# Shared expert of the last two token tiles moved behind the expert loop, and expert 0's weights requested at the head of the output stage

## The reference

```
h   = layer_norm(ALPHA * h + mixer_out @ w_out, ln1_g, ln1_b)      # per token
idx, w = route(h)                                # 6 of 64 experts per token, with weights
routed = sum over the chosen experts e of  w_e * ((silu(h @ wg[e]) * (h @ wu[e])) @ wd[e])
shared = (silu(h @ sg) * (h @ su)) @ sd          # one expert for all tokens
out = layer_norm(ALPHA * h + routed + shared, ln2_g, ln2_b)
```

## Time and profile before

| | us |
|---|---|
| median of 3 runs | 2063.84 (2063.03 to 2066.24) |
| the profiled execution | 2066.02 |
| its span in the profile | 2064.2 |
| PE busy | 1989.3 (96%) |
| DVE busy | 1136.6 (55%) |
| ACT busy | 505.2 (24%) |
| POOL busy | 777.1 (38%) |

### The profile page before, as it was taken

How to read it: one execution, slowest core, us unless ns; L and a number is a source line. 1 busy time by engine, 2 the same in 40 slices (tenths; PEclk the granted TensorE clock), 3 DMA queues, 4 the chain that set the end, 5 groups by cost and what they waited for, 6 DMA issues and landing times.

```text
span 2064.2 us, 23774 instructions
## 1 busy us (share of the span) xinstructions
PE 1989.3 (96%) x7237; PEld 1004.3 (49%) x7238; DVE 1136.6 (55%) x3065; ACT 505.2 (24%) x1102; POOL 777.1 (38%) x717
## 2 busy tenths in 40 slices
PE   8999999999999999999999999999999999999991
PEld 6444667575544444444445554444444444444440
DVE  6222546776611222235676656966666656666645
ACT  3111554452322222224432230111111111111113
POOL 1762005612122222115980003554554545454531
PEclk9999999999999999999999999999999999999996
DMA  5421000011141222144353006999999999999964
GB/s 147 132 87 41 21 21 22 22 47 47 46 138 69 74 77 77 57 130 161 111 202 141 31 32 260 369 364 359 360 360 354 364 346 354 347 342 352 337 206 171
DMA packets 129639, 370.45 MB, mean 179 GB/s; under 512 B 33712, under 2 KB 65668, under 8 KB 103832
## 3 DMA queue, kind: packets, MB, share of 16 engines
q1 hardware_dynamic: 103960, 314.83, 41.1%
q0 software_dynamic: 23520, 54.61, 10.5%
q10 hardware_dynamic: 2080, 0.01, 0.1%
HBM read 320.57 MB, written 68.17 MB: 188 GB/s over the span
## 4 chain that ended last, share of the span: by engine, by line
PE 25%; DMA 21%; issue 4%; POOL 3%; DVE 2%; POOLq 0%; ACT 0%; SPq 0%; DVEq 0%
DMA sums<-arena,row_to 21%; PE banks L3193 8%; PE banks L2289 4%; PE banks L3209 3%; PE banks L2336 3%; POOL arena L2136 2%; PE banks L2014 2%; PE banks L279 1%; PE banks L2352 1%; PE banks L2312 1%; DMA arena<-in_w_router_dram 0%; DVE arena L3269 0%; PE banks L3201 0%; DVE arena L3186 0%; PE banks L2299 0%
## 5 line engine op out<-in xcount | busy, mean ns | idle before, releaser
L3193 PE MATMUL banks<-arena 128*128 128x512 f32 x1056 | 466.6, 595 | 4.1 <-issue 3.5
L3172 POOL DMA_INDIRECT arena<-h_rows,index x268 | 281.0, 1048 | 140.2 <-issue 78.7
L3193 PEld LDWEIGHTS banks<-arena 128*128 128x128 f32 x1056 | 196.6, 191 | 227.7 <-issue 227.6
L1720 PE MATMUL banks<-arena 128*128 128x512 f32 x672 | 298.8, 594 | 0.4 <-ACT arena L323 0.4
L3209 PE MATMUL banks<-arena 128*128 128x512 f32 x528 | 237.5, 592 | 1.4 <-ACT arena L3008 0.9
L3180 POOL DMA_INDIRECT sums<-arena,row_to x66 | 106.2, 1609 | 275.9 <-DMA sums<-arena,row_to 242.2
L279 PE MATMUL banks<-arena 128*128 128x512 f32 x416 | 193.5, 602 | 2.3 <-PEq L108 2.2
L1720 PEld LDWEIGHTS banks<-arena 128*128 128x128 f32 x672 | 123.2, 190 | 134.7 <-issue 134.7
L3156 DVE TENSOR_SCALAR index<-row 32x1 uint32<-32x1 f32 x1072 | 155.4, 145 | 17.1
L3209 PEld LDWEIGHTS banks<-arena 128*128 128x128 f32 x528 | 100.2, 190 | 127.1 <-issue 125.3
L3186 DVE STREAM_TRANSPOSE arena<-arena 128x1024 f32<-128x1024 f32 x66 | 133.7, 2026 | 48.9 <-PE banks L3193 47.2
(11 more groups left out here) (400 smaller groups left out, 2420.0 us busy)
## 6 DMA issues: line engine op xcount, KB each, us to landing
arena<-in_w_exp_gate_dram SPq DMA_DIRECT2D x66, 1024.0 KB, 6.4
arena<-in_w_exp_up_dram SPq DMA_DIRECT2D x66, 1024.0 KB, 10.7
arena<-in_w_exp_down_dram SPq DMA_DIRECT2D x66, 1024.0 KB, 13.5
arena<-in_w_in_dram SPq DMA_DIRECT2D x26, 1024.0 KB, 5.4
gates<-arena SPq DMA_DIRECT2D x60, 256.0 KB, 2.0
arena<-gates SPq DMA_DIRECT2D x15, 1024.0 KB, 7.7
arena<-h_rows,index POOLq DMA_INDIRECT x268
arena<-in_x_dram SPq DMA_DIRECT2D x8, 512.0 KB, 5.6
```

The costliest lines, as they stand in the source:

```text
L1720: mm = pe.matmul(gate_bank(n, b), left[:, k, :], right[:, k, :], start=(alone and k == 0), stop=(k == 3), skip_group_check=True)
L3172: return pool.indirect_dma_start(w.x[k][:, 256 * q:256 * (q + 1)], None, rows, bass.IndirectOffsetOnAxis(ap=g.index[:, k, q:q + 1], axis=0 ...
L3193: mm = pe.matmul(g.bank[:, 2, :].rearrange("p (a f) -> p a f", a=2), xT[:, k, :], wgu[:, :, k, :], start=(k == 0), stop=(k == KT - 1))
```

## The change

`EARLY` is 6. Four things change.

First, the shared expert of tiles 6 and 7 leaves the output stage. Their turned rows are kept in the rows of `base` of tiles 0 and 1, which must have been stored by then (`kept_free`). ACT scales tiles 6 and 7 by ALPHA (`scale`), and SP stores the scaled rows to `sums`. In the final stage PE makes the two tiles: `up` when the last list is there, before the last scatter has landed; then it adds the loaded rows of `sums` in PSUM through a product with the identity matrix, and the `down` products on top. ACT reads these two tiles from PSUM.

Second, SP asks for expert 0's weights ahead of all stores of the output stage, and waits for tile 6 instead of 8 of the shared expert ahead of experts 2 and 3.

Third, the order at the start of the loop is new on PE and DVE. Up of tile 5 is cut in two by the list of expert 0. In step 0 DVE turns expert 1's rows and makes `hidden` ahead of `index`.

Fourth, since the shared weights must stay in `R1` until the end, the overflow tables and the rows of `ln2` lie in the rows of `base` of tiles 2 to 7. So DVE waits ahead of the tables, and SP ahead of loading `ln2`, until all of these have been stored to `sums`.

```diff
@@ norm_and_route, SP
+        load_expert(g, sp, 0)
         for m in range(NT):
             keep_rows(m)
             if m > DELAY:
                 begin_sum(m - DELAY - 1)
         sp.wait_ge(s["mix"], NT)
-        for e in range(2):
-            load_expert(g, sp, e)
-        for m in range(NT - DELAY - 1, NT - 2):
+        load_expert(g, sp, 1)
+        begin_sum(NT - DELAY - 1)
+        for m in range(EARLY, NT):
             begin_sum(m)
-        sp.wait_ge(s["gu"], NT)
+        sp.wait_ge(s["gu"], EARLY)
         load_expert(g, sp, 2)
-        begin_sum(NT - 2)
-        sp.wait_ge(s["dn"], NT)
+        begin_sum(EARLY - 2)
+        sp.wait_ge(s["dn"], EARLY)
         load_expert(g, sp, 3)
-        begin_sum(NT - 1)
+        begin_sum(EARLY - 1)
@@ norm_and_route, PE
-        up(5)
+        up(5, range(0, KT // 2))
         lists(0)
+        up(5, range(KT // 2, KT))
         down(4)
         turn_hidden(5)
-        up(6)
         lists(1)
-        down(5)
-        turn_hidden(6)
-        up(7)
         lists(2)
-        down(6)
-        turn_hidden(7)
-        first.last_down = lambda: down(NT - 1)
+        first.last_down = lambda: down(EARLY - 1)
@@ experts, SP
             first.sync(sp)
+            sp.wait_ge(g.sums_begun, 16 * EARLY)
@@ experts, DVE, step
-                if has(i, c, -1):
+                if not has(i, c, -1):
+                    turned(i, c + 1)
+                    hidden(i, c)
+                    index(i, c + 3)
+                    select(i, c + 4)
+                else:
                     take_rows(i, c - 1)
...
                 if isinstance(i, int) and i == 0:
+                    dve.wait_ge(g.sums_begun, 16 * EARLY)
                     overflow_tables(g, dve, c, then, s["tabled"])
@@ finish, PE (new)
+        pe.wait_ge(v["list"], count)
+        for m in late:
+            for k in range(KT):
+                mm = pe.matmul(bank[:, up_bank[m], :], late_turned(g, m)[:, k, :], wgu[:, k, :],
+                               start=(k == 0), stop=(k == KT - 1))
+            mm.then_inc(s["gu"], 1)
+        for i, m in enumerate(late):
+            pe.wait_ge(s["hid"], i + 1)
+            for k in range(2):
+                mm = pe.transpose(bank[:, up_bank[m], k * P:(k + 1) * P], hid[:, k * P:(k + 1) * P], g.ident[:])
+            mm.then_inc(s["hT"], 1)
+            pe.wait_ge(sum_in[m], 32)
+            for h in range(2):
+                pe.matmul(bank[:, sum_bank[m] + h, :], g.ident[:], z(m)[:, h * HALF:(h + 1) * HALF],
+                          start=True, stop=False)
+            pe.wait_ge(s["hTr"], i + 1)
...
+            mm.then_inc(s["dn"], 1)
@@ finish, ACT
+        late_gate(0)
         for m in range(1, NT):
-            act.wait_ge(sum_in[m], 16)
+            if m == 2:
+                late_gate(1)
+                late_hidden(0)
+            if m == 4:
+                late_hidden(1)
+            if m < EARLY:
+                act.wait_ge(sum_in[m], 32)
+            else:
+                act.wait_ge(s["dn"], m - EARLY + 1)
```

More of the change, by code:

```diff
@@ L2219, in norm_and_route @@
     h1_stored = [sem(f"h1_stored{m}") for m in range(NT)]
+    kept_free = [sem(f"kept_free{i}") for i in range(NT - EARLY)]
     g.sums = nc.dram_tensor("sums", [T, D], F32, kind="Internal").ap()
@@ L2235, in mix_bank @@
         return 6 if m == 1 else 0
-    h_in = [sem(f"h_in{m}") for m in range(NT)]
+    h_in = g.rows_in = [sem(f"rows_in{m}") for m in range(NT)]
     def sync(sp):
@@ L2328, in count, with up @@
             mm.then_inc(s["cnt"], 1)
-        def up(m):
+        def up(m, part=range(KT)):
             if m:
@@ L2334, in up @@
                 pe.wait_ge(s["w"], 48)
-            for k in range(KT):
+            for k in part:
                 mm = pe.matmul(bank[:, up_bank[m], :], h1T(m)[:, k, :], wgu[:, k, :],
                                start=(k == 0), stop=(k == KT - 1))
-            mm.then_inc(s["gu"], 1)
+            if k == KT - 1:
+                mm.then_inc(s["gu"], 1)
         def turn_hidden(m):
@@ L2532, in vector @@
         sum_base(3)
+        index(0)
         hidden(5)
-        index(0)
         select(1)
         sum_base(4)
-        hidden(6)
         index(1)
         select(2)
-        sum_base(5)
         turned_first()
+        index(2)
         select(3)
[L2543 to L2546, removed]
+        first.last_sum = lambda: sum_base(EARLY - 1)
     def scalar(act):
@@ L2588, in scalar @@
         gate(4)
+        for m in range(EARLY, NT):
+            scale(m)
         turned_hidden(4)
@@ L2827, in before @@
                 first.tensor(pe, lambda b: lists(0, b))
-                lists(0, 3)
             def step(i, c):
                 up(i, c)
+                if not has(i, c, -2):
+                    lists(i, c + 3)
                 if has(i, c, -1):
@@ L2835, in step @@
                     first.last_down()
-                if has(i, c, 4):
+                if has(i, c, 4) and has(i, c, -1):
                     lists(i, c + 4)
@@ L2937, in step @@
             def step(i, c):
-                if has(i, c, -1):
-                    take_rows(i, c - 1)
[L2940 to L2946, removed]
+                if not has(i, c, -1):
[4 more added lines that the diff above has]
+                else:
+                    take_rows(i, c - 1)
+                    if has(i, c, 3):
+                        index(i, c + 3)
+                    if has(i, c, 4):
+                        select(i, c + 4)
+                    if has(i, c, 1):
+                        turned(i, c + 1)
+                    hidden(i, c)
                 if has(i, c, -1):
@@ L3119, in expert_work @@
     g.over, g.ovend, g.ones64, g.iota48 = take(NE), take(NE), take(NE), take(48)
-    g.ovef, g.idle, g.ovmore = (g.region(R1 + 3072 + 48 * i, 48) for i in range(3))
+    g.ovef, g.idle, g.ovmore = (g.region(TABLES + 3072 + 48 * i, 48) for i in range(3))
     w.list, w.flag = g.list, g.flag
@@ L3214, in scale_rows, with late_turned, finish @@
 def scale_rows(g):
[L3215 to L3221 removed]
+    return g.region(SCALES, D), g.region(SCALES + D, D)
+def late_turned(g, m):
+    return g.region(KEPT + D * (m - EARLY), KT, P)
+def finish(g, v, ended):
+    sem, bank = g.sem, g.bank
+    at = RING[3] + 2 * D
+    silu, hid, hidT = g.region(at, FF), g.region(at + FF, FF), g.region(at + 2 * FF, 2, P)
+    wgu, wdn = g.region(SHARED, KT, 512), g.region(SHARED + 4096, 2, D)
+    late = range(EARLY, NT)
+    up_bank = {EARLY: 1, EARLY + 1: 0}
+    sum_bank = {EARLY: 6, EARLY + 1: 2}
     g2, b2 = scale_rows(g)
```

83 lines of the change are left out of this document (59 added, 24 removed).

## The result

The changed kernel takes 2075.97 us, median of 4 runs (2075.05 to 2076.3), and the kernel before 2063.44 on the same chip (2062.57 to 2066.24). The ratio is 1.0055, 95% interval [1.0039, 1.0071]. The forecast was 2064.6, about 1 us above the kernel before, with 2056.5 to 2069.5 as its range. The medians are 12.5 us apart, so the direction came out as forecast and the size did not: the time lies 6.5 us above the range. Inside the sum the sign of the larger part is wrong: the loop was to end 4.3 us earlier and ends later.

The account below looks back on a forecast made before the run. PE bounds the output stage; in the loop, the scatters' start and period set the end. Loop -4.3 (-2.3 and 2.0 gained) and final stage +5.1 give +0.8 us: 2064.6 against the 2063.84 median, range 2056.5 to 2069.5.

Parts of the forecast that it names:

- the sign of the larger part: Expert loop: it ends 4.3 us earlier, bounds 0.3 and 7.7.
- The store's landing, and with it the start of the tables: Loop start: tile 5's store lands at 1289.5, DVE waits 7 us, tables start there instead of 1291.8, -2.3 us.
- 1267: Loop start: PE starts expert 0's `up` at 1267, 13 us earlier than 1280.19, not 21.
- the first bound: Loop start: landing of tile 5's store, 2 us either way, each us being one of the loop's start.
- The row of scatters: Expert loop: less early DMA work brings two or three periods from 11.8 to 11.03, 2.0 us gained, bounds 0 and 3.4.
- The rule of the Trainium skill that I cited against this term: Scatters: DMA engines alternate between queues packet by packet, so 3 MB less brings nothing; sum 2.0 us higher.
- The end of the loop: Scatter 61 to 65: no term of its own; the last scatter was to come 4 us earlier.
- The final stage: Behind the loop: two late tiles' shared expert adds 5.1 us, bounds 2.7 and 9.8.
- Tile 2: Final stage: ACT's two table loads, silu and hidden copy make the tiles behind 2.7 us later, bounds 2.7 and 3.3.
- Tile 4: Final stage: ACT waits to copy tile 7's hidden, turned only behind tile 6's `down`; 2.4 us, bounds 0 and 6.5.
- The rivals: Whole kernel: DMA lead kept 2056.4 (15%), full PE gain 2047.6 (5%), slow PE 2069.3 (14%), loop not shorter 2068.6 (6%).
- The slower ones: PE at 1.2 GHz for both late tiles, +5.5 us (14%); loop not shortened at all, +4.8 us (6%).

Follow-up runs that it names:

- the changed kernel's two profiles: The changed kernel profiled once and, unedited, once more beside the other experiments; medians 2075.97 us and 2076.04 us.
- two other profiles with these lines: Changed kernel without tiles 6 and 7's shared expert, 2070.31 us; changed kernel with final loads ordered 0, 1, 6, 2, 7, 3, 4, 5, 2074.63 us.
- the one with late weights: Changed kernel with expert 0's weights asked for behind the wait for the mixes, as in the kernel before; 2075.1 us, ratio 1.0052.
- the first table in DVE's gap: Changed kernel with tables moved, final loads reordered, one table load, plus first overflow-table piece ahead of turning expert 1's rows; 2060.36 us, ratio 0.998.

## Why the prediction was wrong, by its own steps

**The store's landing, and with it the start of the tables: -2.3 forecast, +2.8 measured.** This is the step that failed most, by 5.1 us. Its mechanism is right: DVE waits ahead of the scan, for tile 5's store, behind expert 3, and the row of scatters hangs on the scan. Putting the tables elsewhere took the wait and 9.2 us away; scatter 0 comes 13.95 us behind the scan in before and in after alike. The size is off in three terms, read from the changed kernel's two profiles: expert 0's `up` began 0.5 and 2.3 us later than 1267; it took 8.6 and 8.8 instead of the 6.97 I took, with PE idle ahead of it and a granted clock of 0.82 in the first (9.8 and 10.1 in the two other profiles with these lines); and the landing took 13.4 and 13.2 us instead of 11.8. In the mean these are 1.4, 1.7 and 1.5, and the scan of before was 0.4 earlier in the mean of two profiles than the 1291.8 that I took. That makes 5.0 of the 5.1. The forecast itself said that each microsecond of landing is one of the loop, and put bounds of 2 us on that, though it rested on three estimates in a chain. With the first bound at its worst the row would have moved by -0.3; it moved by +2.8. I had the row of a longer `up` after an idle time and used it for PE's work in the final stage, and not at expert 0, although PE had to stand there: 21.3 us of its work go and the start moves by 13. That 1267 came out to half a microsecond in the first profile is in part luck: the last gather was issued at 1258.13 and not at 1259.7, and its rows took 7.3 us to land where my numbers leave 5.3. Two errors of opposite sign cancelled.

**The row of scatters: -2.0 forecast, 0 measured.** From the scan to scatter 61 it is 703.9 to 706.6 us in all eleven profiles in which the tables keep their place in DVE's list, with the DMA lead and without it, with expert 3's weights sooner or later. So nothing here speaks for a DMA backlog as what makes the early periods long. They may belong to the first steps, in which DVE has the tables to do as well; no run shows that. In before the scatters 1 to 11 take 112.5 us and in the changed kernel 115.2, but counted from scatter 0 it is 126.4 and 126.6. The changed order only moved time from one gap to the next. The rule of the Trainium skill that I cited against this term (DMA: Bandwidth & Descriptors, queues, rings and completion order) named the right sum; the runs agree with it, though they don't show that its mechanism is the reason.

**The end of the loop: no change forecast, +1.3 measured.** In the profile of after the rest block's `up` took 8.82 us against 7.13 before, and the stretch 32.0. In its second profile that `up` took 7.13 and the stretch 28.1. Of all twelve profiles one other has an `up` of 8.82 us there, the one with late weights, and it has the other long stretch, 31.3; in the ten with 7.13 the stretch is 28.0 to 29.8, in before and in changed kernels alike. So I take it as chance of the profile and no effect of the change; the sum of 10.0 counts it all the same.

**The final stage: +5.1 forecast, +5.9 measured (+5.4 over all profiles).** The mechanisms are right, both of them. Tile 2: 2.7 forecast, 2.6 or 2.7 left when tile 4's wait is gone. Tile 4: 2.4 forecast, 3.3 or 2.7 measured. Tile 6's rows landed at 2048.05, 13.5 us behind the first load's issue at 2034.54, where I had 11.4; PE then needed 3.78 + 3.86 = 7.6 us, inside my 7.0 to 8.6. The Trainium skill (ScalarE: Activation LUTs, what a table load costs) would add a drain to each load. After's row shows silu 1.30 us behind the start of its table load and the copy right behind, so no drain is seen, as the trace of before had it.

**The rivals.** None of the four is what happened. The slower ones put +4.8 and +5.5 on the sum, one for a loop that isn't shorter and one for PE at the low clock. What came is a loop that starts later than before, which I had not let in: I bounded the row's move at 0.3 us earlier. The sum with the measured terms is 2.8 + 0 + 1.3 + 5.9 = 10.0, as in the spans. The ratio of the times gives 11 and the medians 12.5; a scan up to 4.9 us late, as in two other profiles with these lines, could make up the rest.

## What to carry to other kernels

When work leaves the bounding engine ahead of a stage, follow the first thing that is now late through every queue, and put it at the sum of its late ends, not at its middle; a chain of one gather, one matmul group at a low clock and one store behind 3 MB ate all 21 us here and 3 more. Before memory is shared between a store and a small table, ask what the wait for the store costs: 9.2 us, against three small arrays of 48 columns placed elsewhere. When two profiles are compared, count from a mark close ahead of the stretch in question; here this took a spread of 4 us out of the readings.

Work that fills an engine's idle time (the tables in DVE's 5 us) is found in the timeline of that engine, not in its busy share.

## What the runs showed of the hardware that I had not expected

A store of 0.5 MB landed 3.7 us after its issue with nothing new ahead of it, and 9.3 us with 3 MB asked for 4.2 us earlier on the same queue; the difference is 5.6 us. And PE's clock: where PE stood 5.24 and 4.65 us with eight small matmuls between, the granted clock was 0.52, near the lower of its two levels (1.2 and 2.4 GHz), and 0.82 in the `up` behind it, which took 8.60 us. In another profile (the first table in DVE's gap), with 5.25 and 5.02 us, that `up` took 9.88. Over the ten profiles of changed kernels it took 8.6 to 10.1.

The start of expert 0's `up` differed by 6.2 us between profiles of kernels that are the same up to there but for expert 0's request (1265.36 to 1271.57), 4.2 us of which stand at the first product of the output stage already, while the two medians of the changed kernel were 2075.97 and 2076.04. One profile of each kernel would have put up to 4 us in the wrong place.
